# Streaming encoder step on one core: order of the first transfers of the opening

## What is computed

```python
def mla_expand(c_kv, k_rope, w_kvup, qk_k_norm):
    kv = (c_kv @ w_kvup).reshape(B, K, MLA_HEADS, MLA_NOPE_DIM + MLA_V_DIM)
    k_nope, v = kv[..., :MLA_NOPE_DIM], kv[..., MLA_NOPE_DIM:]
    kr = jnp.broadcast_to(k_rope[:, :, None, :], (B, K, MLA_HEADS, MLA_ROPE_DIM))
    k = rmsnorm(jnp.concatenate([k_nope, kr], axis=-1), qk_k_norm)
    return k, v

def trunk_layer(x, pos0, lp, rel_bias, past):
    h = rmsnorm(x, lp['norm_mix'])
    proj = h @ lp['w_in']
    ...
    lat_all = jnp.concatenate([past[0], c_kv], axis=1)
    kr_all = jnp.concatenate([past[1], k_rope], axis=1)
    km, vm = mla_expand(lat_all, kr_all, lp['mla_w_kvup'], lp['mla_qk_k_norm'])
    y_mla = mla_attend(qm, km, vm, qpos, kpos)
```

## Time and profile before

| | us |
|---|---|
| median of 3 runs | 1045.88 |
| lowest and highest | 1044.57, 1046.41 |
| span of the profiled execution | 1044.4 |
| TensorE busy | 1037.7 (99%) |
| VectorE, ScalarE, GpSimd busy | 643.6, 506.3, 315.9 |

### The profile page before, as it was taken

One profiled execution on the slowest core, in us unless ns is written; L12 is line 12 of the kernel. 1 busy time (PEld: TensorE's weight loads), 2 busy tenths in 40 slices (PEclk: granted clock), 3 DMA queues, 4 the chain that ended last, 5 costly groups with the idle time before them and its releaser, 6 DMA issues.

```text
span 1044.4 us, 20077 instructions
## 1 busy us (share of the span) xinstructions
PE 1037.7 (99%) x7586; PEld 1004.2 (96%) x7586; DVE 643.6 (62%) x1089; ACT 506.3 (48%) x934; POOL 315.9 (30%) x277
## 2 busy tenths in 40 slices
PE   8999999999999999999999999999999999999998
PEld 6899999999999999999998999999999999999998
DVE  6889754445766566544577986554557565565343
ACT  6457755434554444434365585554445444433341
POOL 3375556531221111100133755655312211111000
PEclk9999999999999999999999999999999999999999
DMA  7465543344535454554513644333354354544541
GB/s 244 103 169 147 167 116 111 100 121 143 160 122 176 146 159 141 152 175 157 164 51 110 171 145 143 95 112 121 122 156 150 121 178 142 157 143 146 156 148 65
DMA packets 48979, 146.29 MB, mean 140 GB/s; under 512 B 8816, under 2 KB 14672, under 8 KB 48912
## 3 DMA queue, kind: packets, MB, share of 16 engines
q1 hardware_dynamic: 42464, 142.86, 44.6%
q10 hardware_dynamic: 6448, 2.50, 0.9%
HBM read 142.11 MB, written 3.22 MB: 139 GB/s over the span
## 4 chain that ended last, share of the span: by engine, by line
PE 97%; DVE 1%; POOL 1%; ACT 0%; issue 0%; ACTq 0%
PE psum L574 29%; PE psum L575 29%; PE psum L576 29%; PE psum L763 1%; PE psum L802 1%; PE psum L785 1%; PE psum L793 1%; PE psum L835 1%; PE psum L1024 0%; PE psum L890 0%; PE psum L925 0%; PE psum L673 0%; PE psum L827 0%; PE psum L743 0%; PE psum L750 0%; PE psum L708 0%
## 5 line engine op out<-in xcount | busy, mean ns | idle before, releaser
L574 PE MATMUL psum<-AH,WH 128*128 128x320 f32 x1328 | 414.6, 312 | 0.2
L576 PE MATMUL psum<-AH,WL 128*128 128x320 f32 x1328 | 410.8, 309 | 0.0
L575 PE MATMUL psum<-AL,WH 128*128 128x320 f32 x1328 | 410.7, 309 | 0.0
L574 PEld LDWEIGHTS psum<-AH,WH 128*128 128x128 f32 x1328 | 249.4, 188 | 7.3 <-issue 5.5
L575 PEld LDWEIGHTS psum<-AL,WH 128*128 128x128 f32 x1328 | 249.5, 188 | 0.2
L576 PEld LDWEIGHTS psum<-AH,WL 128*128 128x128 f32 x1328 | 249.4, 188 | 0.0
L1107 ACT CAST WH<-raw 128x1024 fp32r<-128x1024 f32 x166 | 172.7, 1045 | 125.7 <-PE psum L576 124.6
L1570 DVE TENSOR_TENSOR WL<-raw,WH 128x1024 fp32r<-128x1024 f32 x103 | 128.8, 1252 | 113.3 <-ACT WH L1107 112.9
L2058 POOL TENSOR_TENSOR WL<-raw,WH 128x1024 fp32r<-128x1024 f32 x60 | 147.6, 2477 | 98.2 <-ACT WH L1107 95.5
L1767 DVE TENSOR_TENSOR WL<-raw,WH 128x1024 fp32r<-128x1024 f32 x88 | 107.6, 1222 | 49.5 <-ACT WH L1280 48.1
L2063 POOL TENSOR_TENSOR fab<-fa,fb 128x320 f32<-128x320 f32 x44 | 38.6, 878 | 264.8 <-DVE fb L1772 264.8
(11 more groups left out here) (290 smaller groups left out, 1616.0 us busy)
## 6 DMA issues: line engine op xcount, KB each, us to landing
raw<-w_all SPq DMA_DIRECT2D x264, 512.0 KB, 3.5
y_out<-X SPq DMA_DIRECT2D x8, 160.0 KB, 2.8
X<-x_in SPq DMA_DIRECT2D x2, 320.0 KB, 5.4
X<-x_in SPq DMA_DIRECT2D x1, 640.0 KB, 7.0
lat_out<-ckv ACTq DMA_DIRECT2D x2, 320.0 KB, 2.9
scratch<-brel SPq DMA_DIRECT2D x8, 63.8 KB, 4.5
bias<-scratch SPq DMA_DIRECT2D x8, 48.0 KB, 4.9
ckv<-lat_in ACTq DMA_DIRECT2D x1, 384.0 KB, 4.4
```

The lines of the kernel that those rows point to most:

```text
L574: mm(out, WH[:, slot, c0:c0 + cols], high, start=first, stop=False)
L575: mm(out, WH[:, slot, c0:c0 + cols], low, start=False, stop=False)
L576: return mm(out, WL[:, slot, c0:c0 + cols], high, start=False, stop=last)
```

## The change

SyncE issues the first latents ahead of everything, then the value weights in two transfers of 512 columns each, with a new semaphore `value_half` for the first. ScalarE's first cast waits for `value_half`, its second for `raw_ready[U_KVV]`, which the second transfer now raises. The second latents move from SyncE's queue to ScalarE's. ScalarE issues the rotary keys and the second latents behind its small square root. `WARM` becomes 3.

```diff
-WARM = 4
+WARM = 3
...
+        self.value_half = sem("value_half")
...
-        sp.dma_start(raw[:, U_KVV, :], w_all[stored(U_KVV)]).then_inc(raw_ready[U_KVV], 16)
+        sp.dma_start(ckv[:, :, T:T + 128], lat[:, :, 0:128]).then_inc(s.cache_lat[0], 16)
+        sp.dma_start(raw[:, U_KVV, 0:512], w_all[stored(U_KVV), :, 0:512]).then_inc(s.value_half, 16)
+        sp.dma_start(raw[:, U_KVV, 512:1024], w_all[stored(U_KVV), :, 512:1024]).then_inc(raw_ready[U_KVV], 16)
         sp.dma_start(raw[:, U_KVK, :], w_all[stored(U_KVK)]).then_inc(raw_ready[U_KVK], 16)
-        sp.dma_start(ckv[:, :, T + 128:T + 256], lat[:, :, 128:256]).then_inc(s.cache_lat[1], 16)
...
-        act.dma_start(ckv[:, :, T:T + 128], lat_in[0:1].rearrange("a p c n -> (a p) c n")[:, :, 0:128]) \
-            .then_inc(s.cache_lat[0], 16)
-        act.dma_start(krT[64:96, T:NKEY], kr_in[0:1].rearrange("a p n -> (a p) n")).then_inc(s.cache_kr, 16)
         act.wait_ge(s.warm_zero, 1)
         A(small[:, 31:32], ssum[:, 0:1], ACT.Sqrt)
-        act.wait_ge(raw_ready[U_KVV], 16)
+        act.dma_start(krT[64:96, T:NKEY], kr_in[0:1].rearrange("a p n -> (a p) n")).then_inc(s.cache_kr, 16)
+        act.dma_start(ckv[:, :, T + 128:T + 256], lat_in[0:1].rearrange("a p c n -> (a p) c n")[:, :, 128:256]) \
+            .then_inc(s.cache_lat[1], 16)
         for c in range(2):
+            act.wait_ge(raw_ready[U_KVV] if c else s.value_half, 16)
             half = slice(512 * c, 512 * c + 512)
             nc.scalar.copy(WKH[:, U_KVV, half], raw[:, U_KVV, half]).then_inc(s.first_high, 1)
```

## The result

The changed kernel is slower: 1048.01 us median (1046.29 to 1050.36, 9 runs) against 1045.18 us (1044.14 to 1046.41, 9 runs) in the same study, a recorded ratio of 1.0023 (95% interval 1.0015 to 1.0031; the two medians alone give 1.0027). So it is about a quarter of a per cent slower. I had forecast 1044.6, in a range of 1043.2 to 1046.6.

What follows compares the result with a forecast made beforehand. TensorE was taken as the bound, losing 1.2 us early to late latents, with key weights a second bound. Earlier key-weight subtractions (1.0) plus a vanished stall (0.3) took 1.3 us off the 1045.88 median: 1044.6 us, range 1043.2 to 1046.6.

Steps and rivals of the forecast that it cites:

- What bounds the kernel now: Opening: TensorE is the bound, waiting 1.2 us before the value rows for late latents; key weights are a second bound.
- The first term: VectorE's key-weight subtractions, no longer queued behind the value ones, end at 8.4 instead of 9.41: 1.0 us gained.
- I take 6.4: Key weights' landing, given 6.0 to 7.6, taken as today's 6.40 because the bytes in front are the same or fewer.
- Rival A: Key weights or second latents land late and become the new wait; gain only 0.2 to 0.6 us, 1045.5; chance 0.24.
- Rival C: TensorE stays at the lower clock beyond the value rows; slower, 1047.5 to 1050 us; chance 0.05.
- the loss of a warm-up matmul: Opening of TensorE: three warm-up matmuls end at 4.75 instead of 5.9; worth 0 to 0.2 us, counted 0.
- The latents' landing: First latents, first on SyncE's queue, land between 3.5 and 6.25 us, taken as 3.7; a second estimate gave about 3.0.
- ScalarE's queue: Table load and square root go first; rotary keys and second latents leave at about 2.8 and 3.4, costing nothing or 0.1 us.
- The stall: VectorE's 96 x 1 product, 1.23 us through exclusion with GpSimd's subtraction, passes freely after the change: 0.3 us counted.
- The sum and the span: 1.0 + 0.3 = 1.3 us gained in the opening, a shift that stays to the end of the 1044.4 us span.

Runs made afterwards that it cites:

- e13: The kernel before, unchanged, traced once more: latents cast at 4.69 us instead of 6.25.
- e7: The change with the value weights in one transfer and four warm-up matmuls instead of three: 1046.11 us, ratio 1.0007.
- e5: The change with five warm-up matmuls instead of three: 1046.54 us, ratio 1.0013.
- e1: The change with four warm-up matmuls instead of three: 1047.69 us, ratio 1.0021.
- e11: The change with whole value weights, four warm-up matmuls, and rotary keys and second latents behind the key weights on SyncE's queue: 1046.16 us, ratio 1.0006.
- e9: The kernel before with VectorE's two small key-gain products of the first layer moved to idle time before the first sum of squares: 1044.77 us, ratio 0.9997.
- e16: The edit of e9 to the kernel before, run once more: 1044.55 us, ratio 0.9998.
- e2: The kernel before with three warm-up matmuls instead of four: 1046.74 us, ratio 1.0011.
- e14: The change, unchanged, traced once more: key weights cast at 8.13 us, span 1045.5 us.

## Why the prediction was wrong

- **What bounds the kernel now: right for the trace, wrong for the kernel.** TensorE waits for the latents in that one execution. In the usual one it waits for the key weights, and by the ruler the span is then 1042.4 to 1044.2 (cast at 6.42 to 7.34, 2.34 more to the turning, and one of the two constants); the first trace, at 1044.4, is near the slow end of that kernel's executions (1042.4 to 1044.7 but for six of 120). The first term, 1.0 us, came from 9.41 - 8.4 on VectorE; usually those subtractions are not queued behind anything (e13: the turning 2.34 us behind the cast) and there was nothing to gain.
- **"I take 6.4": the failed step.** I gave the key weights 6.0 to 7.6 and took 6.4 because fewer bytes stood in front. They were cast at 7.79, 8.13 and, with the same transfers, 7.78 and 8.65. The 5.2 us from issue to landing that I had called queueing stayed at least 5.2 from an issue 1.4 us later. The bytes in front were not fewer, since the second latents left 0.9 us ahead of the key weights, and the flow was not 394 GB/s but 241 from 4 to 5 us. The same step failed for the value weights: I had the whole landing near 4.7, and the second half was cast at 6.49. Rival A had this mechanism, with a gain left over; it is a loss, since its price was set against the slow trace (e7, without any fall of the clock, is 0.7 us slower than the kernel before). Latents on SyncE's queue account for 0.7 us (e7), the halves in that order for 0.4 more (e5 less e7; the two medians' difference, with one warm-up matmul more in e5, so roughly).
- **Rival C, the clock: right in kind, with 0.05.** It is the larger part by the medians, 1.5 us (the change less e5); by the two traces with the same cast it is 1.1. I argued against it that the pause between warm-up and work shrinks to 0.2 us. But the first pause was 0.8, since the first half was cast at 4.81 instead of 4.4, and I had not looked at the second: cutting the value weights cuts TensorE's first work in two, with 0.9 us of waiting between. I also counted the loss of a warm-up matmul as 0; in the order of before it is 1.4, in the changed order 0.3 (the change less e1). One sum of this rival is off too: half of the 5.5 us, less 1.3, gives 1047.3 and not 1047.5.
- **The latents' landing: right.** I took 3.7; in the seven traces with them first on SyncE's queue they were cast at 3.33 to 3.96. The other estimate, about 3.0, was low.
- **ScalarE's queue:** the table load started at 0.74 and both issues were out by 2.35, earlier than I had them (2.8 and 3.4), so that the square root stood in nobody's way. The early issue put the second latents in front of the key weights; e11, which takes them away again, gained 0.3 us at the cast and nothing in the time, so they are not the whole of it.
- **The stall: mechanism right, size wrong.** I counted 0.3 us for its end; the ruler says 0.8, and e9 and e16 agree. It did not end in the change, because both engines moved together (15.04 on GpSimd, 15.19 on VectorE).
- **The sum and the span:** that a shift in the opening stays to the end held in all eighteen traces, once the stall is told apart: the distance from the turning to the end varies by 0.1 to 0.2 us.

Together: 0.7 (order) + 0.4 (halves) + 1.5 (clock) = 2.6 us. That these add up to the difference proves nothing, since each is the step from one median to the next (before, e7, e5, the change), with up to 0.5 us of doubt each. The clock's 1.5 is the least sure. The changed kernel has nine executions, and its median one stands 2.7 us above its own span, where its other eight stand 1.8 to 1.9. By the medians of the spans (1043.6, 1044.3, 1044.7 and 1045.7) the same three steps are 0.7, 0.4 and 1.0, together 2.1.

## What to carry to other kernels

Before removing a wait of a microsecond, trace a second execution of the same kernel: here one landing at 6.25 us, usually at 4.7, was the whole case for the change. Splitting a transfer so that an engine can start sooner also splits the engine's work, and here TensorE, with pauses in between, lost its clock in about half of the executions, for more than the early start could gain; follow the pauses up to the next long piece of work and fill them with matmuls if need be. Where several transfers share the engines, judge a new order by when the last needed one lands, not the first: here the latents came 0.7 us sooner than usual (3.96 against 4.7) and the key weights over a microsecond later.

## What the runs showed of the hardware

- The clock's record isn't complete at the start: windows read 1.00 in e2 and e14 while 512-column matmuls started 0.43 us apart instead of 0.23. A fall, once the clock had risen, is recorded as 0.50 (the change, 8 to 11 us).
- Warm-up work has a step here: 0, 3, 4 and 5 matmuls of 1.16 us in the same kernel gave 1046.98, 1046.74, 1045.39 and 1045.32 us.
- The key weights' transfer, issued second to fourth on its queue, was cast 5.2 to 6.1 us behind its issue in all eighteen traces, though its place in the queue and its neighbours differed; the same 128 KB of latents in the same place were cast between 4.66 and 6.25 us from one execution to another.
- One product of 96 x 1 on VectorE that meets GpSimd's subtraction takes 1.23 us instead of 0.15 (e13), and this kernel then takes 0.8 us longer.
